# Multiplying the first projection unit in two halves of its features, around the modulation's second half

## The reference, cut to what matters

```python
ada = silu(c) @ w_ada[0] + b_ada[0]            # six rows of 1024: shift1, scale1, gate1, shift2, scale2, gate2
h   = rmsnorm(x, norm1_g[0]) * (1 + scale1) + shift1
z   = h @ w_in[0]                              # 1024 -> 7200 columns, cut into q/kv ranks, heads and gates
```

## Time and profile before

| | us |
|---|---|
| median of three runs (1743.43 to 1746.32) | 1745.09 |
| the profiled execution | 1743.61 |
| its span, first to last instruction | 1741.9 |
| TensorE busy | 1684.2 |
| VectorE busy | 1180.3 |
| ScalarE busy | 857.8 |
| GpSimd busy | 147.1 |

### The profile page before, as it was taken

How to read it: one execution, slowest core, us unless ns; L and a number is a source line. 1 busy time by engine, 2 the same in 40 slices (tenths; PEclk the granted TensorE clock), 3 DMA queues, 4 the chain that set the end, 5 groups by cost and what they waited for, 6 DMA issues and landing times.

```text
span 1741.9 us, 24848 instructions
## 1 busy us (share of the span) xinstructions
PE 1684.2 (97%) x9315; PEld 1389.8 (80%) x9315; DVE 1180.3 (68%) x2033; ACT 857.8 (49%) x1505; POOL 147.1 (8%) x296
## 2 busy tenths in 40 slices
PE   6999999999999999999999999999999999999998
PEld 3887785689878886774899878767998787679986
DVE  5776565866776975547735676666788767667885
ACT  3354463455443442661555354575554544755542
POOL 1210101000000000210000010041000100410000
PEclk8999999999999999999999999899999999999999
DMA  9887335557855974337465646604665566046552
GB/s 344 294 283 263 122 97 167 191 195 249 297 156 192 347 252 164 121 98 231 147 213 186 194 144 224 175 1 156 196 187 185 162 214 185 1 144 207 182 184 83
DMA packets 185912, 323.71 MB, mean 186 GB/s; under 512 B 13540, under 2 KB 101184, under 8 KB 185792
## 3 DMA queue, kind: packets, MB, share of 16 engines
q1 hardware_dynamic: 183200, 320.54, 56.5%
q10 hardware_dynamic: 2592, 1.57, 0.3%
HBM read 321.02 MB, written 1.05 MB: 185 GB/s over the span
## 4 chain that ended last, share of the span: by engine, by line
PE 71%; DVE 15%; ACT 5%; DMA 3%; issue 3%; POOL 2%; SPq 0%; DVEq 0%; POOLq 0%; ACTq 0%
PE bank L741 67%; DVE ring_r L1813 6%; PE bank L750 3%; ACT sm L1458 2%; DMA ring<-in_w_in 1%; DMA ring<-in_w_ada 1%; POOL sm L667 1%; DVE ada L1918 1%; ACT high L1372 1%; DVE gates_r L1838 1%; DVE sm L1998 1%; DMA ring<-in_w_ff 1%; DVE oT L1882 0%; DVE gates L2496 0%; DVE oT_r L1845 0%
## 5 line engine op out<-in xcount | busy, mean ns | idle before, releaser
L1813 DVE TENSOR_TENSOR ring_r<-ring,high 128x1024 fp32r<-128x1024 f32 (+3 forms) x390 | 460.5, 1197 | 266.1 <-ACT high L1372 258.1
L1372 ACT ACTIVATE high<-ring 128x1024 fp32r<-128x1024 f32 (+3 forms) x390 | 402.0, 1037 | 480.2 <-PE bank L741 353.4
L741 PE MATMUL bank<-ring_r,featT_r 128*128 128x512 f32 (+3 forms) x928 | 354.9, 382 | 0.0
L741 PE MATMUL bank<-high,featT_r 128*128 128x512 f32 (+3 forms) x712 | 276.5, 388 | 8.3 <-DVE oT_r L1845 2.6
L741 PE MATMUL bank<-featT_r,high 128*128 128x256 f32 x960 | 272.9, 284 | 0.0
L741 PE MATMUL bank<-featT_r,ring_r 128*128 128x256 f32 x960 | 271.6, 283 | 0.0
L741 PE MATMUL bank<-oT_r,high 128*128 128x256 f32 x960 | 271.6, 283 | 0.0
L741 PE MATMUL bank<-high,oT_r 128*128 128x512 f32 (+3 forms) x712 | 270.1, 379 | 0.0
L741 PE MATMUL bank<-high,gates_r 128*128 128x512 f32 x736 | 230.2, 391 | 3.6 <-DVE ring_r L1813 2.6
L741 PEld LDWEIGHTS bank<-ring_r,featT_r 128*128 128x128 f32 x928 | 175.5, 189 | 27.0 <-issue 0.5
L741 PEld LDWEIGHTS bank<-oT_r,high 128*128 128x128 f32 x960 | 184.2, 192 | 0.6 <-issue 0.5
(11 more groups left out here) (267 smaller groups left out, 2204.7 us busy)
## 6 DMA issues: line engine op xcount, KB each, us to landing
ring<-in_w_ff SPq DMA_DIRECT2D x128, 512.0 KB, 4.6
ring<-in_w_ada SPq DMA_DIRECT2D x96, 512.0 KB, 5.8
ring<-in_w_up SPq DMA_DIRECT2D x176, 256.0 KB, 3.5
ring<-in_w_in SPq DMA_DIRECT2D x64, 464.0 KB, 5.3
ring<-in_w_in SPq DMA_DIRECT2D x48, 512.0 KB, 5.2
ring<-in_w_in SPq DMA_DIRECT2D x48, 474.0 KB, 4.8
ring<-in_w_down SPq DMA_DIRECT2D x44, 512.0 KB, 3.4
ring<-in_w_out SPq DMA_DIRECT2D x24, 512.0 KB, 4.7
```

The source lines that it names most:

```text
L741: ins = pe.matmul(o, a, b, start=start, stop=stop, skip_group_check=True)
L1372: act.activation(it["high"], it["raw"], ACT.Copy).then_inc(high_ready, 1)
L1813: dve.tensor_tensor(it["low"], it["raw"], it["high"].bitcast(F32), ALU.subtract).then_inc(low_ready, 1)
```

## The change

Four things change, all in layer 0 of the first block.

- **Stream.** Two pieces of unit 0 stand between the modulation's halves (ahead of the fifth pair of w_ada pieces), and the other two behind the last w_ada piece.
- **PE.** In half 1 of the modulation, after its first piece, PE multiplies chunks 0 to 3 of unit 0 for both token tiles (24 matmuls), then goes on with pieces two to four; chunks 4 to 7 (24 matmuls) come after half 1. Both tiles' banks stay open between; tile 0 uses a bank of `for_act` and no longer one of `outputs`.
- **ACT.** Two high parts stand ahead of `features_out` and two between it and the second `gain_out`. After the second `evac_dve` ACT applies gain and shift to chunks 4 to 7 of tile 1 and rounds them, ahead of `late_rows`. It also copies unit 0's result for tile 0 out, after unit 1's high parts and `late_small`.
- **DVE.** Two low parts and the low parts of chunks 0 to 3 come before half 1's four `ada_step`s, the other two low parts before the second `both_out`; then chunks 4 to 7 of tile 0 alone, and for tile 1 only the low part.

```diff
@@ the stream
-                for it in pe_ada:
+                begun = [cols_piece(w_in[l], k0, k0 + 2, (0, ATT_W), split=True) for k0 in range(0, KD, 2)]
+                for n, it in enumerate(pe_ada):
+                    if n == 4:
+                        for j in range(2):
+                            put(begun[j], spare_1[j], True, 12)
+                    if n == 5:
+                        for j in range(2):
+                            used(begun[j])
                     put(it)
                     ada_piece()
+                for j in range(2, 4):
+                    put(begun[j], spare_1[j], False, 12)
+                split_units.append(begun)
+                low_units.append(begun)
...
             for u in range(11):
+                if u == 0 and l == 0:
+                    continue
@@ PE
-            def tokens_as_ready(second=None):
+            def tokens_in_halves():
                 get, n = next_quarters()
...
+                rings = for_act, for_dve
+                open_ = [claim(r)[0] for r in rings]
+
+                def half_of(i):
+                    for t in range(T):
+                        for j in (2 * i, 2 * i + 1):
+                            w = get(j)
+                            for kk in range(2):
+                                c = 2 * j + kk
+                                features(c, [t])
+                                three(open_[t][:, 0:n], feature_parts(c, slice(t * P, t * P + P)), (w[0][:, kk, :], w[1][:, kk, :]),
+                                      c == 0, c == KD - 1, rings[t].full if c == KD - 1 else None)
+                            if t:
+                                owed.append((piece_used, 1))
+
+                return half_of
...
-                    modulation_pair(1)
-                    tokens_as_ready()
+                    halves = []
+
+                    def first_half():
+                        halves.append(tokens_in_halves())
+                        halves[0](0)
+
+                    modulation_pair(1, first_half)
+                    halves[0](1)
@@ ACT
+            def last_features(gain, shift):
+
+                act.wait_ge(for_dve.full, 2)
+                for f in range(4, 8):
+                    ins = act.activation(featF[:, f, P:2 * P], for_dve.banks[1][:, (f - 4) * P:(f - 3) * P], ACT.Identity,
+                                         scale=gain[:, f:f + 1], bias=shift[:, f:f + 1])
+                link(ins)
+                act.wait_ge(for_dve.read, 1)
+                act.sem_inc(for_dve.read, 1)
+                act.activation(featT_r[:, 4:8, P:2 * P], featF[:, 4:8, P:2 * P], ACT.Copy).then_inc(feat_high, 1)
...
                     gain_out(0)
+                    highs(2)
                     seen.more(evac_dve)
                     features_out(gain, shift, True)
+                    highs(2)
                     gain_out(1)
-                    highs(4)
                     seen.more(evac_dve)
+                    last_features(gain, shift)
                     late_rows()
...
                     highs(4)
-                    if u < (2 if l else 1):
-                        if l == 0:
-                            late_small()
+                    if u < 2 and l:
                         continue
+                    if u == 0:
+                        late_small()
                     b = tile()
@@ DVE
                     for half_ in range(2):
+                        if half_:
+                            first_quarters(2)
+                            for t in range(T):
+                                first_lows(t)
                         for j in range(4):
                             ada_step()
...
                         if half_:
-                            for t in range(T):
-                                first_lows(t)
-                            first_quarters(1)
+                            first_quarters(2)
                         both_out(half_)
                         dve.sem_inc(evac_dve, 1)
-                    last_features(gain, shift, 0)
-                    first_quarters(1)
-                    last_features(gain, shift, 1)
-                    first_quarters(2)
+                    last_features(gain, shift)
+                    last_lows()
...
-                    if u == 0:
-                        b = tile(outputs)
-                        read(outputs, dve.tensor_copy(proj[:, 0, c0:c0 + n], b[:, 0:n]))
```

More of the change, by code:

```diff
@@ L1855, in first_lows, with last_lows, last_features @@
                                   ALU.subtract).then_inc(feat_first, 1)
-            def last_features(gain, shift, t):
-                cols = slice(t * P, (t + 1) * P)
+            def last_lows():
+                got[id(for_dve)] += 1
+                seen.more(feat_high)
+                dve.tensor_tensor(featL[:, 4:8, P:2 * P], featF[:, 4:8, P:2 * P], featT_r[:, 4:8, P:2 * P].bitcast(F32),
+                                  ALU.subtract).then_inc(feat_last, 1)
+            def last_features(gain, shift):
+                cols = slice(0, P)
                 b = tile(for_dve)
```

## The result

The changed kernel takes 1746.95 us, the median of 20 runs (1743.58 to 1752.59); the kernel before, timed beside it, 1744.74 (20 runs, 1740.87 to 1747.90). The medians differ by 2.2 us. The measured ratio, which is not the quotient of the two medians (1.0013), is 1.0019 with a 95% interval of 1.0012 to 1.0025, or 2.1 to 4.4 us: the change costs time, and the ratio is at the edge of the 0.2% that I had called no change.

What follows compares the result with a forecast made beforehand. PE, busy 97% of the span, was taken as the bound, with savings only before unit 1. The early half's saving was given back by the later modulation and ACT's issues: +0.04 us, median 1745.1 us, range 1742.3 to 1748.3.

Steps and rivals of the forecast that it cites:

- case A: No change: unit 0's end and ACT's chain both near 50 us, 1744.4 to 1746.1 us; chance 0.5.
- rival C: Slower: clock falls already in unit 0's first half, matmuls spaced by 0.388 us; 1746.5 to 1749.8, likeliest 1747; chance 0.19.
- rival D: Unit 0's fourth piece lands 2 us later, everything behind moves by 2: 1747; sign, row copy after 38 us; chance 0.08.
- mark for mark: The change is costed by the start of unit 1 on PE, at 49.91 us in the kernel before.
- First half, 25.6 to 30.6: Unit 0's first 24 matmuls on PE, at the full clock, 0.208 us each, 5.0 us together.
- Rest of the modulation: Three remaining w_ada pieces on PE take 5.31 us after the first half, ending at 35.9 us against 29.5 before.
- SP and the fourth piece: SP waits for slots; unit 0's fourth piece, issued about 31.6, lands at 35.6 us; modulation's signal at 39.0 against 33.6.
- Second half: Unit 0's last 24 matmuls start at 41.65 us, take 5.0 to 9.3 us, end about 48.8.
- ACT behind it: `late_rows` starts 1.65 us after the signal, its issues take 7.15; unit 1's first high part starts at 47.8 us.
- -1.1 us: The sum if ACT's `late_rows` issues held up nothing and unit 1 started when PE is free.
- The sum: Unit 1 at 49.95 us against 49.91, so +0.04 us on the profiled 1743.61; stated as a median, 1745.1.
- What moves at no cost: DVE gets slack, unit 2's pieces are issued before 38 us instead of at 46.53, nothing past unit 2 changes.

Runs made afterwards that it cites:

- a_rows: Changed kernel with ACT's 18 `late_rows` DMAs moved behind unit 1's high parts: 1745.42 us, ratio 1.0006 to the kernel before.
- a_sp: Changed kernel with the 18 `late_rows` DMAs issued by SP instead of ACT: 1745.22 us, ratio 1.0001 to the kernel before.
- a_row_first: Changed kernel with ACT's row copy and DVE's `both_out` ahead of the high and low part of unit 0's fourth piece: 1747.30 us, ratio 1.0013 to the kernel before.
- a_repeat: Changed kernel run once more, unaltered: 1746.95 us, ratio 1.0011 to the kernel before.
- a_warm: Changed kernel with PE's idle gaps in the modulation filled by products that nobody reads: 1746.97 us, ratio 1.0013 to the kernel before.
- b_help: Kernel before with ACT applying gain and shift to tile 1's chunks 4 to 7, and `late_rows` behind unit 1's high parts: 1745.37 us, ratio 1.0000 to it.
- b_sp_warm: Kernel before, unit 0 in one, with unread products in PE's gaps and `late_rows` on SP: 1741.67 us, ratio 0.9981 to the kernel before.
- b_warm: Kernel before, unit 0 in one, with only unread products added in PE's gaps: 1741.35 us, ratio 0.9984 to the kernel before.
- a_sp_all: Changed kernel with row copy and `both_out` ahead of the fourth piece, unread products in PE's gaps, `late_rows` on SP: 1741.82 us, ratio 0.9985 to the kernel before.
- a_all: Changed kernel with row copy and `both_out` ahead of the fourth piece, unread products in PE's gaps, `late_rows` behind unit 1's high parts: 1743.79 us, ratio 0.9999 to the kernel before.

## Why the prediction was right, and what was mis-sized in it

I had given most weight to a change within 0.2%, and at 1.0019 it lies just inside; the value is 1.9 us above mine (1746.95 against 1745.1), inside the range. The chain of waits was right, and ACT's issues were its last link. But case A, which carried the value, did not happen: the sum came out at nothing, and the kernel is slower, by terms that I had named but sized too small or left to the rivals. Two of the signs that I had listed as "wrong" came true, C's spacing of 0.39 us and D's row copy after 38 us (39.6 and 38.5). That the time is inside the range owes something to luck: by my own rule, mark for mark, the first trace's 53.59 would have made 1748.8 us, outside it, and the second's 52.22 1747.4. Point by point:

*First half, 25.6 to 30.6.* The start was right to 0.1 us. The 24 matmuls took 6.9 us and not 5.0, because the clock was low for the first ten. That was rival C's outcome, with 0.19 too low a chance: it happened in both traces of the changed kernel and in a_rows and a_sp, and only a_row_first of the changed kernels without filling matmuls escaped. C's reason, the gap from 23.7 to 25.6, fits a_repeat, where the clock fell after a gap of 1.92 us. In the first trace it had fallen before any such gap (0.69 granted from 22 to 24 us), right behind the 16 tiny matmuls of half 0. In the kernel before a fall there is nearly free.

*Rest of the modulation.* 5.31 us for three pieces and no wait for DMA, as forecast, from 32.6 instead of 30.6. The order of what waits for what was right: the weights waited for PE.

*SP and the fourth piece (rival D too).* The term was mis-sized. The second issue came at 33.66 instead of 31.6, since the first half ended later, and took 5.0 us to land where the row for the empty queue said 4.0: 38.7 instead of 35.6. The signal came at 42.0 and not 39.0. By the trace, PE's pieces ended 2.0 us late (37.9 against 35.9), and the other 1.0 is the piece's; I had 0.3 for it in the 39.0. In a_repeat the piece landed at 37.6 and cost only some 0.2 (signal at 41.0), so that the 5.0 us to landing belong to one execution, while the issue 2 us late is in both.

*Second half.* PE started 2.8 us after the signal, at the low clock, and took 7.5 us, inside the 5.0 to 9.3.

*ACT behind it.* This is the step that the runs bear out best. From signal to the first cast of unit 1 I had 8.8 us (1.65 + 7.15); it was 9.3, the 18 issues taking 7.6. a_rows and a_sp took them away, and their medians are 1.5 and 1.7 us lower; a_warm let PE finish early, and it waited 3.34. The Trainium skill's sentence that a sequencer's time to initiate a DMA is usually small relative to the DMA itself (DMA: Bandwidth & Descriptors, "Issuing engines are not separate DMA queues") I had read as if the issues held up nothing, which gave -1.1 us. The sentence is about one DMA, and this trace agrees with it: `late_small`'s first one took 0.41 us to issue and 3.7 to land. It was my reading that failed, since 18 issues add up to 7.6 us in ACT's program, ahead of a cast that PE waits for.

*The sum.* 3.0 us for the signal and 0.5 for the issues, with 0.1 of steps between, make 53.6 of 49.95, the first trace's mark. The mark's other side moves too: the kernel before starts unit 1 at 49.9 or 51.2, with 16 or 24 of unit 0's spacings at the low clock. I had taken one trace's mark for the kernel's. Two traces of each are too few to say how the medians' 2.2 us follow from the marks.

*What moves at no cost.* Right: no unit after unit 1 waited more than before, and unit 2's pieces were in early. The value of such slack is open: b_help, without it, lost its earlier unit 1 at unit 3, while b_sp_warm, also without it, kept its own.

What stays open: the worth in time of the fourth piece's delay (a_row_first), where b_warm saves its 3 us, and whether the halves give anything that the filled gaps alone don't (a_sp_all and b_sp_warm can't be told apart). The halves as such were not tried with SP's wait removed, since the ring's slots force it.

## What to carry to other kernels

When half of a unit is moved ahead of the step that releases everything else, cost first what that step's other followers do afterwards: here the modulation's end came 7 to 8 us later and dragged along a block of small DMAs that had been cover. The 18 small DMAs that ScalarE issued cost it about 0.4 us each in program order (7.15 and 7.6 us together); give such issues to a queue that idles, as a_sp did. And before rearranging work to fill a gap in front of matmuls, try filling it with matmuls that nobody reads: in the kernel before it brought 3 us with no change of order. In the changed kernel it brought nothing by itself (a_warm), where by its trace PE then waited for ACT's issues.

## What the hardware showed that I had not expected

- The place where TensorE's clock falls differs from one execution to the next of the same kernel. In the changed kernel it is low from between 22 and 24 us in one trace (behind 16 one-column matmuls, with 0.30 us of idling ahead of them) and from 27.5 in the other (after an idle gap of 1.92 us). The kernel before falls once near 34 us in one trace, and in the other a first time between 22 and 24. Two traces of one kernel differ by 1.3 to 1.4 us at unit 1.
- Filling PE's gaps with unread products mostly kept it up: unit 0 has at most 3 spacings of 0.3 to 0.6 us out of 47 in the six kernels that fill them, against 23 and 18 in the traces of the changed kernel and 16 and 24 in those of the kernel before. Over all executions the mean granted clock is 0.991 to 0.992 in these six, and 0.988 to 0.990 in the others but a_row_first (0.991). It doesn't rule a fall out: a_all shows 0.50 from 24 to 26 us, where PE runs mostly the unread products.
- Two pieces of the same 464 KB, issued 2 us apart into a nearly empty queue, took 3.5 and 5.0 us to land in one execution and 3.4 and 3.8 in another (a_repeat).
